# Sliding-window attention: the value matmuls with V stationary in two column halves, reciprocals spread by transfers

## The chip, the cores and the metric

The kernel runs on one core of a Trainium2 chip. The time is that of the whole program on the device, in microseconds (us); a kernel's time is the median of its runs.

## What is computed

One layer of a hybrid transformer for 2048 prompt tokens and 64 decode tokens, all in float32: input projections, latent attention (8 heads), sliding-window attention (8 query heads, 2 key/value heads of 64), output projection, and a convolutional feed-forward. The change touches the sliding attention alone:

```python
def swa_attend(q, k, v, bias, sinks, mask):
    s = jnp.einsum('bcqhgd,bckhd->bhgcqk', q, k).astype(jnp.float32) * SWA_SCALE + bias[:, :, None]
    if mask is not None:
        s = jnp.where(mask, s, NEG_INF)
    sink = sinks.astype(jnp.float32).reshape(SWA_KV_HEADS, SWA_GROUP, 1, 1, 1)
    m = jnp.maximum(jnp.max(s, axis=-1, keepdims=True), sink)
    e = jnp.exp(s - m)
    p = e / (jnp.sum(e, axis=-1, keepdims=True) + jnp.exp(sink - m))
    return jnp.einsum('bhgcqk,bckhd->bcqhgd', p.astype(v.dtype), v)
```

Each chunk of 64 queries sees its own 64 keys and the 128 before. The sum of the exponentials and the sink make the denominator of each query and head.

## The kernel before, in words

The program is a row of blocks: `project_inputs`, `window_attention`, `latent_attention`, `mix_and_ffn`. In each block every engine has a program of its own, written out by hand, and the engines meet at semaphores alone; a block begins when all engines have ended the one before.

`window_attention` (from line 781) walks over 17 tiles of queries: tiles 0 to 15 of 128 prompt tokens, tile 16 of the 64 decode tokens. A tile has 256 keys (192 for decode), in two halves of 128. Buffers of a tile alternate by its parity p. `walk` (line 852) sets the order on every engine: step t is `front(t)`, then `back(t-1)` (on ScalarE `back(t-1)`, then `front(t)`), and behind it `tail(t-2)`; steps 2 to 15 are a hardware loop of two steps and an unrolled pair.

- SP, `front`: loads queries, keys and V (transposed) of tile t+1, once the scores of tile t-1 and the turn of tile t's V are done. `tail`: stores a tile's output (line 918) once ScalarE has copied it.
- TensorE, `front` (line 950): scores of the 8 heads, queries stationary, 8 matmuls with 64 rows, in pairs in the upper and the lower half of the rows. Each fp32 matmul is two passes, which the profile lists as two instructions. `back` (line 974): in four groups g of two heads, four transposes of the probabilities each (into bank g % 2 of `tr`), and one group later the four value matmuls of the group (line 1002): the turned probabilities are stationary, V moves, 64 columns. Then V of the next tile is turned (line 972), and `tail` turns the finished output (line 1013).
- ScalarE, `front` (line 1024): eight exponentials with their sums (line 1028), one for the sink. `back` (line 1039): copies the four groups of turned probabilities from PSUM (line 1042), then the turned V (line 1037). `tail`: copies the turned output (line 1049).
- VectorE, `front` (line 1063): four instructions scale the scores and add the bias (line 1068), then the maximum (line 1076), its negative (1079) and the sink's offset (1082). `back`: denominator (1087), reciprocal (1089), and the product of values and reciprocals from PSUM (1092).
- GpSimd only sets constants (from line 938).

What waits for what around the change: `tr` has two banks and `ov`, `tt` one buffer each; the turned V and the turned output share `tt`. The product at 1092 waits for all value matmuls of a tile, and the next tile's value matmuls wait for it.

## Time and profile before

| | us |
|---|---|
| median of 3 runs (lowest, highest) | 2946.76 (2939.91, 2949.11) |
| the profiled execution's own time | 2937.64 |
| span of its trace, first to last instruction | 2935.8 |
| TensorE busy | 2773.2 (94%) |
| VectorE, ScalarE, GpSimd busy | 1888.1, 1316.3, 298.2 |
| mean granted clock of TensorE | 0.974 |
| sliding attention | 369.5 to 577 |

How to read the views: a row of the timeline begins with its start and its length in us (merged rows: from the first start to the last end), then engine, line, operation, output<-inputs, sizes and xcount; in brackets the time that the engine was idle before it and what ended that. PEld is TensorE's weight load, which overlaps PE. A row of the windows view has the stretch, its length, then busy time and (xcount) of PE, PEld, VectorE, ScalarE and GpSimd, the granted clock as a share of 2.4 GHz, the busy share of the DMA engines, and GB/s. A row of the source view has the least, the median and the greatest length in ns. A row of the DMA view has the bytes of one transfer and the median time from its issue to its landing in us.

### The profile page before, as it was taken

How to read it: one execution, taken by the hardware profiler on the slowest of the kernel's cores; microseconds unless marked ns; L12 is line 12 of the kernel's file. 1: busy time of each engine (PE TensorE's matmuls, PEld its weight loads, DVE VectorE, ACT ScalarE, POOL GpSimd, SP SyncE). 2: the span in 40 equal slices, each digit the busy share in tenths (PEclk: the TensorE clock that was granted, in tenths of full speed). 3: DMA queues.
4: the chain of work that ended last, by engine and by line, in shares of the span. 5: the costliest groups of instructions: out<-in, count | busy, mean ns of one | idle time of the engine just before them, and what ended most of it. 6: DMA issues, size and time to landing. Idle time of an engine off the chain costs nothing.

```text
span 2935.8 us, 43437 instructions
## 1 busy us (share of the span) xinstructions
PE 2773.2 (94%) x13872; PEld 2487.7 (85%) x13872; DVE 1888.1 (64%) x2662; ACT 1316.3 (45%) x2744; POOL 298.2 (10%) x336
## 2 busy tenths in 40 slices
PE   8999968799999998899999999999999999999996
PEld 7899857666666667799999989999899999999996
DVE  6777646466666673777647873487644876458743
ACT  5434246533333343464435444354434545346532
POOL 1111010000000001300010002100021101201002
PEclk9999979899999999999999999999999999999998
DMA  7566552313332213234333443335333353333432
GB/s 221 199 225 209 188 142 72 75 23 70 73 66 55 54 46 115 77 114 138 119 104 108 138 155 118 99 110 169 116 120 102 115 179 114 120 100 114 140 123 74
DMA packets 162016, 344.87 MB, mean 117 GB/s; under 512 B 41636, under 2 KB 105860, under 8 KB 160228
## 3 DMA queue, kind: packets, MB, share of 16 engines
q1 hardware_dynamic: 161892, 343.25, 38.7%
q8 instruction: 73, 1.20, 0.2%
q14 instruction: 51, 0.42, 0.0%
HBM read 288.83 MB, written 55.23 MB: 117 GB/s over the span
## 4 chain that ended last, share of the span: by engine, by line
PE 54%; DVE 2%; issue 2%; ACT 1%; DMA 1%; POOL 1%; SPq 0%; POOLq 0%; ACTq 0%; DVEq 0%
PE mf_acc L1877 53%; DVE mix_w_lo L2030 1%; ACT mix_w_hi L1923 1%; DMA mix_w_raw<-in_w_up 1%; POOL mf_ss L1835 1%; PE mf_st L1915 0%; DVE mf_x L2048 0%; DMA mix_w_raw<-in_w_out 0%; DVE mf_xn L2081 0%; DVE mf_x L2053 0%; POOL mf_y L1860 0%; DVE mix_a_lo L2086 0%; ACT mf_sq L1946 0%; ACT mf_sq L1980 0%; DVE mf_rstd L2065 0%
## 5 line engine op out<-in xcount | busy, mean ns | idle before, releaser
L2030 DVE TENSOR_TENSOR mix_w_lo<-mix_w_raw,mix_w_hi 128x1024 fp32r<-128x1024 f32 (+1 forms) x338 | 471.3, 1395 | 557.9 <-ACT mix_w_hi L1923 557.1
L1877 PE MATMUL mf_acc<-mix_a_hi,mix_w_hi 128*128 128x424 f32 (+1 forms) x2016 | 725.1, 360 | 29.3 <-DVE mix_a_lo L2060 8.8
L1877 PE MATMUL mf_acc<-mix_a_hi,mix_w_lo 128*128 128x424 f32 (+1 forms) x2016 | 718.6, 356 | 0.0
L1877 PE MATMUL mf_acc<-mix_a_lo,mix_w_hi 128*128 128x424 f32 (+1 forms) x2016 | 717.6, 356 | 0.0
L1923 ACT ACTIVATE mix_w_hi<-mix_w_raw 128x1024 fp32r<-128x1024 f32 (+1 forms) x338 | 382.2, 1131 | 520.4 <-PE mf_acc L1877 492.6
L1877 PEld LDWEIGHTS mf_acc<-mix_a_hi,mix_w_hi 128*128 128x128 f32 x2016 | 382.1, 190 | 45.0 <-issue 12.1
L1877 PEld LDWEIGHTS mf_acc<-mix_a_hi,mix_w_lo 128*128 128x128 f32 x2016 | 382.4, 190 | 10.8
L1877 PEld LDWEIGHTS mf_acc<-mix_a_lo,mix_w_hi 128*128 128x128 f32 x2016 | 382.3, 190 | 9.3 <-issue 0.7
L1345 PE MATMUL la_sc<-ahead_q,ahead_k 97*128 97x512 f32 (+5 forms) x1008 | 361.8, 468 | 0.0
L1877 PE MATMUL mf_acc<-mf_h_hi,mix_w_hi 128*128 128x424 f32 (+1 forms) x944 | 339.7, 360 | 6.8 <-DVE mix_w_lo L2030 3.9
L1877 PE MATMUL mf_acc<-mf_h_hi,mix_w_lo 128*128 128x424 f32 (+1 forms) x944 | 335.9, 356 | 0.0
L1877 PE MATMUL mf_acc<-mf_h_lo,mix_w_hi 128*128 128x424 f32 (+1 forms) x944 | 335.3, 355 | 0.0
L1407 ACT ACTIVATE la_prob<-la_sc 128x512 f32<-128x512 f32 (+1 forms) x336 | 174.1, 518 | 314.5 <-PE la_sc L1345 313.9
L1361 PE MATMUL la_ov<-la_prob,ahead_v 128*128 128x512 f32 (+5 forms) x672 | 293.5, 518 | 0.0
L1345 PEld LDWEIGHTS la_sc<-ahead_q,ahead_k 97*128 97x128 f32 (+1 forms) x1008 | 180.5, 189 | 128.5 <-issue 95.2
L1460 DVE TENSOR_REDUCE la_part<-la_sx 128x1 f32<-128x512 f32 (+5 forms) x328 | 184.6, 574 | 162.3 <-PE la_sx L1322 159.1
L1835 POOL TENSOR_TENSOR mf_ss<-mf_sq,mf_ss 128x424 f32<-128x424 f32 (+1 forms) x105 | 145.5, 1385 | 478.1 <-ACT mf_sq L1946 347.9
L1877 PEld LDWEIGHTS mf_acc<-mf_h_hi,mix_w_hi 128*128 128x128 f32 x944 | 178.3, 189 | 14.6 <-DVE mix_w_lo L2030 5.0
L1877 PEld LDWEIGHTS mf_acc<-mf_h_lo,mix_w_hi 128*128 128x128 f32 x944 | 178.2, 189 | 5.9 <-issue 1.7
L1877 PEld LDWEIGHTS mf_acc<-mf_h_hi,mix_w_lo 128*128 128x128 f32 x944 | 178.1, 189 | 4.2
L749 PE MATMUL pi_acc<-pi_x_hi,pi_w_hi 128*128 128x424 f32 (+1 forms) x400 | 148.0, 370 | 19.6 <-DVE pi_x_lo L528 14.5
L2104 DVE SCALAR_TENSOR_TENSOR mf_cv<-mf_u,mf_conv_w,mf_cv 128x424 f32<-128x424 f32 (+1 forms) x220 | 145.0, 659 | 32.5 <-DVE mf_cv L2101 28.9
(187 smaller groups left out, 3664.2 us busy)
## 6 DMA issues: line engine op xcount, KB each, us to landing
mix_w_raw<-in_w_up SPq DMA_DIRECT2D x220, 512.0 KB, 3.6
mix_w_raw<-in_w_down SPq DMA_DIRECT2D x80, 704.0 KB, 4.1
pi_w_raw<-in_w_in SPq DMA_DIRECT2D x49, 512.0 KB, 6.0
mix_w_raw<-in_w_out SPq DMA_DIRECT2D x40, 512.0 KB, 3.6
ahead_k<-kn_scr SPq DMA_DIRECT2D x8, 1120.0 KB, 14.8
ahead_q<-qn_scr SPq DMA_DIRECT2D x8, 1056.0 KB, 8.0
pi_x_raw<-in_x SPq DMA_DIRECT2D x4, 1696.0 KB, 11.4
qn_scr<-pi_ring SPq DMA_DIRECT2D x16, 424.0 KB
```

Of the source, the lines that this page charges most:

```text
L749: mm = pe.matmul(acc[:, g, 0:n], w[:, s, k], x[:, par, k, 0:n], start=(k == 0 and m == 0), stop=(k == KD - 1 and m == 2))
L1345: mm = pe.matmul(out, k[0:KR, p, a, c0:c0 + keys], q[0:KR, p, b, n0 + off:n0 + n], start=(term == 0), stop=(term == 2))
L1361: pe.matmul(ov[:, (5 * p + pos) % 2, off:n], v[0:keys, p, vt], prob[0:keys, (NKT * p + s) % RING, off:n], start=(m == 0), stop=(s == last_ ...
L1407: act.activation(prob[0:keys, (NKT * p + s) % RING, off:n], sc[0:keys, s % 3, off:n], ACT.Exp, scale=MLA_SCALE).then_inc(exp_done, 1)
L1460: op = dve.tensor_reduce(part[0:rows, par, t, slot:slot + 1], sx[0:rows, bank, 0:seen], AX_X, ALU.max)
L1835: pool.tensor_tensor(ss[:, kind, 0:n], sq[:, slot, 0:n], zeros[:, 0:n] if first else ss[:, kind, 0:n], ALU.add).then_inc(sq_added, 1)
L1877: mm = pe.matmul(acc[:, t_bank[0], 0:n], w[:, g, k], x[:, k, 0:n], start=(first and k == 0 and m == 0), stop=(last and k == count - 1 and ...
L1923: act.activation(w_hi[:, g, 0:count], w_raw[:, g, 0:count], ACT.Copy).then_inc(w_hi_made, 1)
L2030: dve.tensor_tensor(w_lo[:, g, 0:count], w_raw[:, g, 0:count], w_hi[:, g, 0:count].bitcast(F32), ALU.subtract).then_inc(w_split, 1)
L2104: dve.scalar_tensor_tensor(out=out, in0=u[:, g, 1:n + 1], scalar=conv_w[:, 1, bass.ds(f, 1)], in1=out, op0=ALU.mult, op1=ALU.add).then_inc ...
```

## The change

Cut to its core. Left out are semaphores that only change their names or are merged (`neg_done` and `off_done` into `shift_done`, and the like).

- Values: `values` at line 1005 of the new kernel makes a tile's output with four matmuls instead of sixteen. V is stationary, 128 keys by 64 columns, for key/value head g at columns 64g to 64g+63 of the array, and the turned probabilities of that head's four queries' heads move, 512 columns. The output comes out turned, [64g.., 4, 128], so the four output transposes and ScalarE's copy of them are gone.
- The turned probabilities are now grouped by key/value head and half, c = 2g + half, into bank `half` of `tr`. VectorE copies the first of the four groups (`keep_first`), ScalarE the other three.
- The reciprocals of a tile [128 queries, 8] are turned by TensorE into rows [8, 128], copied to SBUF by VectorE, written to DRAM by SP, and, when that has landed, read back twice with a step of 0 over 64 partitions (`spread`). VectorE copies the values from PSUM, and GpSimd multiplies them by the spread reciprocals (`scale`). `store` waits for that and is two transfers instead of one.
- TensorE's turn of the next V waits for `rec_kept`, VectorE's copy of the turned reciprocals, and `values` for `ov_kept`, VectorE's copy of the values before.

```diff
+            def spread(t, p, n):
+                sp.wait_ge(rec_kept, t + 1)
+                sp.dma_start(d["rec_scr"][p][:, 0:n], rec_rows[:, p, 0:n]).then_inc(rec_out[p], 16)
+                sp.wait_ge(rec_out[p], 16 * nth(t, p) + 16)
+                for g in range(2):
+                    row = bass.AP(tensor=d["rec_scr"].tensor, offset=(p * HEADS + g * SWA_GROUP) * P,
+                                  ap=[[0, SWA_DIM], [P, SWA_GROUP], [1, n]])
+                    sp.dma_start(rec_all[g * SWA_DIM:(g + 1) * SWA_DIM, p, :, 0:n], row).then_inc(rec_in[p], 16)
+
             def store(t, p, n):
-                sp.wait_ge(out_copied, t + 3)
+                sp.wait_ge(normed, t + 1)
                 cols = bass.ds(t * P, P) if n == P else slice(SEQ, TOK)
-                sp.dma_start(d["att_swa"][:, :, cols], outT[:, p, :, 0:n]).then_inc(att_out[p], 16)
-
-            def nothing(t, p, n):
-                pass
+                for g in range(2):
+                    sp.dma_start(d["att_swa_rows"][g][:, :, cols],
+                                 outT[g * SWA_DIM:(g + 1) * SWA_DIM, p, :, 0:n]).then_inc(att_out[p], 16)
...
+
+            def scale(t, p, n):
+                pool.wait_ge(ov_kept, t + 1)
+                pool.wait_ge(rec_in[p], 32 * nth(t, p))
+                if not (isinstance(t, int) and t == 0):
+                    pool.wait_ge(normed, t)
+                pool.tensor_tensor(outT[:, p, :, 0:n], outT[:, p, :, 0:n], rec_all[:, p, :, 0:n],
+                                   ALU.mult).then_inc(normed, 1)
+
+            pool.wait_ge(rows_set, 6)
+            walk(pool, nothing, scale, nothing)
+
...
             def turn_v(t, p, n):
                 if not (isinstance(t, int) and t == 0):
-                    pe.wait_ge(out_copied, t)
+                    pe.wait_ge(rec_kept, t)
                     pe.wait_ge(v_copied, t)
-                if not isinstance(t, int) or t > 0:
                     pe.wait_ge(qkv_in[p], 48 * nth(t, p) if n == P else 48 * (NT // 2) + 64)
                 pe.transpose(tt[0:n, 0, :], v_t[:, p, 0:n], ident[:]).then_inc(v_turned, 1)
 
+            def turn(t, p, n, g, half):
+
+                keys = DEC if half and n == DEC else P
+                for i in range(SWA_GROUP):
+                    mm = pe.transpose(tr[0:keys, half, i, 0:n],
+                                      prob[0:n, p, SWA_GROUP * g + i, half * P:half * P + keys], ident[0:n, 0:n])
+                mm.then_inc(tr_done, 1)
+
+            def values(t, p, n, half):
+
+                keys = DEC if half and n == DEC else P
+                src = ((v[:, 1 - p], v[:, p]) if n == P else (v_cache, v_new))[half]
+                for g in range(2):
+                    rows = slice(g * SWA_DIM, (g + 1) * SWA_DIM)
+                    mm = pe.matmul(ov[rows, :, 0:n], src[0:keys, rows], probT[0:keys, 2 * g + half, :, 0:n],
+                                   start=(half == 0), stop=(half == 1), skip_group_check=True)
+                if half:
+                    mm.then_inc(ov_done, 1)
+
             def back(t, p, n):
-                keys = (P, P if n == P else DEC)
-                for g in range(4):
-                    pe.wait_ge(exp_done, 8 * t + 2 * g + 2)
-                    pe.wait_ge(tr_copied, 4 * t + g + 1)
-                    for m in range(4):
-                        half = m % 2
-                        mm = pe.transpose(tr[0:keys[half], g % 2, m, 0:n],
-                                          prob[0:n, p, 2 * g + m // 2, half * P:half * P + keys[half]],
-                                          ident[0:n, 0:n])
-                    mm.then_inc(tr_done, 1)
-                    if g >= 1:
-                        values(t, p, n, keys, g - 1)
-                values(t, p, n, keys, 3)
+                pe.wait_ge(exp_done, 8 * t + 4)
+                pe.wait_ge(tr_copied, 3 * t + 2)
+                turn(t, p, n, 0, 0)
+                pe.wait_ge(tr_copied, 3 * t + 3)
+                turn(t, p, n, 0, 1)
+                pe.wait_ge(exp_done, 8 * t + 8)
+                pe.wait_ge(tr0_copied, t + 1)
+                turn(t, p, n, 1, 0)
+                pe.wait_ge(tr_copied, 3 * t + 4)
+                turn(t, p, n, 1, 1)
+                pe.wait_ge(v_copied, t + 1)
+                if not (isinstance(t, int) and t == 0):
+                    pe.wait_ge(ov_kept, t)
+                if n == DEC:
+                    pe.wait_ge(bias_in[1], 32)
+                pe.wait_ge(tr_copied, 3 * t + 5)
+                values(t, p, n, 0)
+                pe.wait_ge(tr_copied, 3 * t + 6)
+                values(t, p, n, 1)
+                pe.wait_ge(rec_done, 2 * t + 2)
+                pe.transpose(tt[0:HEADS, 1, 0:n], rec[0:n, p], ident[0:n, 0:n]).then_inc(rec_turned, 1)
                 if n == P:
                     turn_v(t + 1, 1 - p, P if not (isinstance(t, int) and t == NT - 1) else DEC)
 
-            def values(t, p, n, keys, g):
-                pe.wait_ge(tr_copied, 4 * t + g + 3)
-                if g == 0:
-                    pe.wait_ge(normed, t + 1)
-                    pe.wait_ge(v_copied, t + 1)
-                    if n == DEC:
-                        pe.wait_ge(vcache_in, 16)
-                for m in range(4):
-                    h, half = 2 * g + m // 2, m % 2
-                    kv = h // SWA_GROUP * SWA_DIM
-                    src = ((v[:, 1 - p], v[:, p]) if n == P else (v_cache, v_new))[half]
-                    mm = pe.matmul(ov[0:n, h], probT[0:keys[half], g, m, 0:n],
-                                   src[0:keys[half], kv:kv + SWA_DIM], start=(half == 0), stop=(half == 1))
...
-                pe.wait_ge(normed, t + 2)
-
-                pe.wait_ge(v_copied, NT + 1 if isinstance(t, int) and t > NT - 2 else t + 3)
-                pe.wait_ge(out_copied, t + 2)
-                for m in range(4):
-                    mm = pe.transpose(tt[:, m, 0:n], out[0:n, p, 2 * m:2 * m + 2].rearrange("p a b -> p (a b)"),
-                                      ident[0:n, 0:n])
-                mm.then_inc(out_turned, 1)
...
-            def keep_v(t, p, n):
+
+            def back(t, p, n):
                 act.wait_ge(v_turned, t + 1)
                 act.activation((v[:, p] if n == P else v_new)[0:n], tt[0:n, 0, :], ACT.Copy).then_inc(v_copied, 1)
-
-            def back(t, p, n):
-                for g in range(4):
-                    act.wait_ge(tr_done, 4 * t + g + 1)
-                    act.activation(probT[:, g], tr[:, g % 2], ACT.Copy).then_inc(tr_copied, 1)
-                if n == P:
-                    keep_v(t + 1, 1 - p, P if not (isinstance(t, int) and t == NT - 1) else DEC)
-
-            def tail(t, p, n):
-                act.wait_ge(out_turned, t + 1)
-                act.wait_ge(att_out[p], 16 * nth(t, p))
-                act.activation(outT[:, p, :, 0:n], tt[:, :, 0:n], ACT.Copy).then_inc(out_copied, 1)
-
-            walk(act, front, back, tail, back_first=True)
+                for c in range(1, 4):
...
+            def keep_first(t):
+                dve.wait_ge(tr_done, 4 * t + 1)
+                dve.tensor_copy(probT[:, 0], tr[:, 0]).then_inc(tr0_copied, 1)
 
...
                     dve.scalar_tensor_tensor(out=prob[0:n, p, h:h + 2, 0:keys], in0=sc[0:n, q, :, 0:keys],
                                              scalar=SWA_SCALE, in1=bias[0:n, p, h:h + 2, 0:keys],
                                              op0=ALU.mult, op1=ALU.add).then_inc(biased, 1)
+                if not (isinstance(t, int) and t == 0):
+                    keep_first(t - 1)
                 dve.wait_ge(biased, 4 * t + 8)
...
             def back(t, p, n):
+                if n == DEC:
+                    keep_first(t)
                 dve.wait_ge(exp_done, 8 * t + 8)
                 dve.wait_ge(sink_done, t + 1)
-                dve.tensor_tensor(den[0:n, p], total[0:n, p], sink_exp[0:n, p], ALU.add).then_inc(den_done, 1)
-                dve.wait_ge(den_done, t + 1)
+                dve.tensor_tensor(den[0:n, p], total[0:n, p], sink_exp[0:n, p], ALU.add).then_inc(rec_done, 1)
+                dve.wait_ge(rec_done, 2 * t + 1)
                 dve.reciprocal(rec[0:n, p], den[0:n, p]).then_inc(rec_done, 1)
-                dve.wait_ge(rec_done, t + 1)
+                dve.wait_ge(rec_out[p], 16 * nth(t, p))
+                dve.wait_ge(rec_turned, t + 1)
+                dve.tensor_copy(rec_rows[:, p, 0:n], tt[0:HEADS, 1, 0:n]).then_inc(rec_kept, 1)
                 dve.wait_ge(ov_done, t + 1)
-                dve.tensor_tensor(out[0:n, p], ov[0:n],
-                                  rec[0:n, p].rearrange("p (h o) -> p h o", o=1).broadcast_to([n, HEADS, SWA_DIM]),
-                                  ALU.mult).then_inc(normed, 1)
+                dve.wait_ge(att_out[p], 32 * nth(t, p))
+                dve.tensor_copy(outT[:, p, :, 0:n], ov[:, :, 0:n]).then_inc(ov_kept, 1)
...
+    d["rec_scr"] = nc.dram_tensor("rec_scr", (2, HEADS, P), F32, kind="Internal").ap()
+    d["att_swa_rows"] = [d["att_scr"][4 + 2 * g:6 + 2 * g].rearrange("k (e c) t -> c (k e) t", e=2) for g in range(2)]
```

The order of one step on TensorE, inside the loop (`wa_sc` scores, `wa_tr` turned probabilities, `wa_ov` values, `wa_tt` turned V, output or reciprocals). Before:

```order
L958 MATMUL wa_sc<-wa_k,wa_q 128x256 x4
...
L981 MATMUL wa_tr<-ahead_ident,wa_prob 128x128 x4
...
L1002 MATMUL wa_ov<-wa_vtok,wa_probT 128x64 x4
...
L981 MATMUL wa_tr<-ahead_ident,wa_prob 128x128 x4
...
L1002 MATMUL wa_ov<-wa_vtok,wa_probT 128x64 x4
L972 MATMUL wa_tt<-ahead_ident,wa_v 128x128
...
L1013 MATMUL wa_tt<-ahead_ident,wa_out 128x128 x4
```

Now:

```order
L982 MATMUL wa_sc<-wa_k,wa_q 128x256 x4
L1017 ISA
L1018 ISA
L1001 MATMUL wa_tr<-ahead_ident,wa_prob 128x128 x4
...
L1032 REGISTER_ALU
L1011 MATMUL wa_ov<-wa_probT,wa_vtok 64x512 x2
L1034 REGISTER_ALU
L1011 MATMUL wa_ov<-wa_probT,wa_vtok 64x512 x2
L1036 ISA
L1037 MATMUL wa_tt<-ahead_ident,wa_rec 8x128
L995 MATMUL wa_tt<-ahead_ident,wa_v 128x128
```

Before, groups of transposes and of values alternate and the output transposes end the step; now all sixteen transposes stand ahead of all values, and a turn of the reciprocals stands between the values and the turn of V.

The order of one step on VectorE, inside the loop, in the new kernel (`wa_rec_rows` turned reciprocals, `wa_outT` values to be multiplied):

```order
L1089 SCALAR_TENSOR_TENSOR wa_prob<-wa_sc,wa_bias 128x512
L1081 ISA
L1082 COPY wa_probT<-wa_tr 128x512
L1094 REGISTER_ALU
L1099 TENSOR_REDUCE wa_top<-wa_prob 128x8
...
L1112 TENSOR_TENSOR wa_den<-wa_total,wa_sink_exp 128x8
L1113 ISA
L1114 RECIPROCAL wa_rec<-wa_den 128x8
L1115 ISA
L1117 COPY wa_rec_rows<-wa_tt 8x128
L1119 REGISTER_ALU
L1120 COPY wa_outT<-wa_ov 128x512
```

The copy of the first group stands ahead of the maximum, and the two copies at the end stand where the product was (L1092 before).

The order of one step on SP's queue, inside the loop, in the new kernel:

```order
L893 DMA wa_q<-q_scr 128x4x128
L894 DMA wa_k<-k_scr 128x256
L895 DMA wa_v<-v_scr 128x128
L917 DMA rec_scr<-wa_rec_rows 8x128
L918 ISA
L922 DMA wa_rec_all<-rec_scr 64x512 x2
...
L928 DMA att_scr<-wa_outT 64x4x128
L928 ISA
L928 DMA att_scr<-wa_outT 64x4x128
```

Before, the three loads are followed by one store; now the write of the reciprocals, the wait for it, and the two reads stand between them.

## Rows read from the trace of the kernel before

**Rows 1.** Windows view, 20 us of the sliding attention in full swing

```profile
475.00:495.00 20.00, 16.56 (x139) 14.44 (x139) 12.33 (x20) 13.78 (x46) 0.00 (x0) 1.00 0.25 68
```

**Rows 2.** Timeline: starts of bias additions, and the next stage's first row

```profile
408.25 1.29 DVE L1068 SCALAR_TENSOR_TENSOR wa_prob<-wa_sc,wa_bias 128x512 f32<-128x512 f32 x2 [6.55 <-PE wa_sc L958]
...
468.85 2.48 DVE L1068 SCALAR_TENSOR_TENSOR wa_prob<-wa_sc,wa_bias 128x512 f32<-128x512 f32 x4 [1.49 <-PE wa_sc L958]
...
550.90 1.94 DVE L1068 SCALAR_TENSOR_TENSOR wa_prob<-wa_sc,wa_bias 64x384 f32<-64x384 f32 x4 [1.18 <-PE wa_sc L958]
...
577.05 0.18 POOL L1295 MEMSET la_part<- 128x24 f32 x2 [194.02 <-POOLq L786]
```

**Rows 3.** Timeline of ScalarE over one round

```profile
466.72 0.28 ACT L1037 ACTIVATE wa_vtok<-wa_tt 128x128 f32<-128x128 f32 x1 [1.31 <-PE wa_tt L972]
...
471.40 1.06 ACT L1042 ACTIVATE wa_probT<-wa_tr 128x512 f32<-128x512 f32 x2
...
473.62 0.60 ACT L1042 ACTIVATE wa_probT<-wa_tr 128x512 f32<-128x512 f32 x1 [1.16 <-PE wa_tr L981]
...
474.90 0.60 ACT L1042 ACTIVATE wa_probT<-wa_tr 128x512 f32<-128x512 f32 x1 [0.68 <-PE wa_tr L981]
...
476.81 0.28 ACT L1037 ACTIVATE wa_vtok<-wa_tt 128x128 f32<-128x128 f32 x1 [1.31 <-PE wa_tt L972]
```

**Rows 4.** Timeline of TensorE: the scores of tile 2, then one round

```profile
406.14 3.78 PE L958 MATMUL wa_sc<-wa_k,wa_q 64*128 64x256 f32 x16 [5.03 <-DMA wa_v<-v_scr]
...
467.05 0.66 PE L1013 MATMUL wa_tt<-ahead_ident,wa_out 128*128 128x128 f32 x4 [0.37 <-ACT wa_vtok L1037]
...
467.69 2.00 PE L958 MATMUL wa_sc<-wa_k,wa_q 64*128 64x256 f32 x16
...
472.86 0.48 PEld L981 LDWEIGHTS wa_tr<-ahead_ident,wa_prob 128*128 128x128 f32 x4
...
474.70 1.95 PE L1002 MATMUL wa_ov<-wa_vtok,wa_probT 128*128 128x64 f32 x16
...
476.38 0.20 PEld L972 LDWEIGHTS wa_tt<-ahead_ident,wa_v 128*128 128x128 f32 x1
```

**Rows 5.** Timeline of VectorE in the same round

```profile
471.37 2.29 DVE L1076 TENSOR_REDUCE wa_top<-wa_prob 128x8 f32<-128x2048 f32 x1
...
474.29 0.20 DVE L1089 RECIPROCAL wa_rec<-wa_den 128x8 f32<-128x8 f32 x1
...
476.76 0.69 DVE L1092 TENSOR_TENSOR wa_out<-wa_ov,wa_rec 128x512 f32<-128x512 f32 x1 [2.27 <-PE wa_ov L1002]
```

**Rows 6.** Timeline of TensorE in the latent attention, fp32 passes of 512 columns

```profile
710.18 1.02 PE L1361 MATMUL la_ov<-la_prob,ahead_v 128*128 128x512 f32 x2
...
711.97 0.59 PE L1361 MATMUL la_ov<-la_prob,ahead_v 128*128 128x512 f32 x1
```

**Rows 7.** Source view of line 554, VectorE's copies of 512 columns from PSUM

```profile
L554 DVE COPY pi_ring<-pi_ex x21: 680/683/692, 128.6 to 365.8; 106x512 f32<-106x512 f32 x16, 104x512 f32<-104x512 f32 x4, 128x512 f32<-128x512 f32 x1
```

**Rows 8.** Windows around the clock's fall; then the maximum's starts around it

```profile
533.00:534.00 1.00, 1.00 (x9) 1.00 (x8) 1.00 (x1) 0.01 (x1) 0.00 (x0) 0.70 0.84 236
...
529.80:532.60 2.80, 1.42 (x13) 0.89 (x9) 2.77 (x5) 2.80 (x12) 0.00 (x0) 1.00 0.00 0
...
531.86 2.29 DVE L1076 TENSOR_REDUCE wa_top<-wa_prob 128x8 f32<-128x2048 f32 x1
...
543.60 2.29 DVE L1076 TENSOR_REDUCE wa_top<-wa_prob 128x8 f32<-128x2048 f32 x1
```

**Rows 9.** DMA view, transfers like those that the change adds

```profile
wa_q<-q_scr SPq DMA_DIRECT2D x16, 256.0 KB, 2.9
...
ahead_v<-vt_scr SPq DMA_DIRECT2D x8, 16.0 KB, 10.5
...
att_scr<-la_att SPq DMA_DIRECT2D x8, 16.0 KB, 1.7
```

**Rows 10.** Source view of line 1835, GpSimd's sums of two inputs

```profile
L1835 POOL TENSOR_TENSOR mf_ss<-mf_sq,mf_ss x105: 1059/1104/2128, 1147.3 to 2912.3; 128x424 f32<-128x424 f32 x84, 128x416 f32<-128x416 f32 x21
```

More of the change, by code:

```diff
@@ L1007, in tail, with nothing @@
[L1007 to L1017 removed]
+            def nothing(t, p, n):
+                pass
```

78 lines of the change are left out of this document (40 added, 38 removed).

## The prediction

> **What bounds the kernel now.** I first looked for the stage that the change touches. The windows view [rows 1] gives the sliding attention in full swing: of 20 us TensorE has matmuls in flight for 16.6, ScalarE is busy 13.8 and VectorE 12.3, at a granted clock of 1.00. No engine is full, so the period of a tile is set by a ring of waits. The timeline of VectorE [rows 2] marks the tiles by the first of the four instructions that add the bias: tile 2 starts at 408.25, the last one (64 decode tokens) at 550.90, so 14 steps take 142.65 us, and the stage ends at 577.05 when the next one's first memset runs. Everything outside 408 to 577 I leave as it is.
>
> The ring is on ScalarE [rows 3]. The copy of the turned V starts in one round at 466.72 and in the next at 476.81: 10.09 us. Between them the eight exponentials run without a gap, then the copy of the output tile, then four copies of turned probabilities, before which ScalarE waits 1.16, 0.68 and, for the turned V, 1.31 us: 3.15 us idle per round. What it waits for is TensorE [rows 4], whose value matmuls are sixteen, one for each head and half of the keys, each in two fp32 passes with a stationary load: the last 16 of the 32 passes alone take 1.95 us. VectorE [rows 5] is waiting too (2.27 us before its product). So the present period is ScalarE's 6.9 us of work plus TensorE's share in between.
>
> **The change, part by part.** I follow one step of the new order, from the start of the bias additions to the next start, because VectorE now stands in three places of one ring: it copies the first turned quarter, it has to finish the reciprocals before TensorE may turn them, and TensorE may not turn the next V (same PSUM tile) before VectorE has taken the turned reciprocals away.
>
> 1. Bias additions to their end, 468.85 to 471.37 [rows 2, 5]: 2.52.
> 2. New: VectorE copies quarter 0 from PSUM, 128x512: 0.69 [rows 7]; it stands ahead of the 2.3 us maximum, and TensorE's quarter 2 reuses that bank, so it is on the path. Handing over 0.05.
> 3. TensorE turns quarter 2 (four transposes) until ScalarE starts: 472.86 to 473.62, 0.76 [rows 3, 4].
> 4. ScalarE copies it: 0.60 [rows 3]. Quarter 3 follows half a copy behind and is hidden by the first value matmuls. Handing over and changing the array's layout: 0.13.
> 5. The values. Before, 32 passes; now 8 passes of 512 columns. A pass of this kind in the latent attention takes 1.02 - 0.59 = 0.43 us from start to start [rows 6]. One after another, 8 take 3.44. If the two column halves run side by side, only the order of issue binds (first half's two passes, then its second beside the other's first): 5 x 0.43 = 2.15. I take 2.15, since the scores, whose two row halves are issued the same way, already do this: 16 passes of 256 columns in 2.00 us [rows 4], under 0.13 each, where half of 0.43 would be 0.215. No row shows column halves, so 3.44 stays as the upper end; nothing suggests less than 1.72. The Trainium skill (TensorEngine Tiling (Array Packing), Key Properties) says different tiles run independently; its TensorE: Matmul & The Clock Gate, Part 3, gives 2.38x for three column tiles. By that factor, taken as 1.6x for two, the term would be an estimated 2.2. The same page on tiling says that changing the layout drains the array; no row here isolates that.
> 6. TensorE turns the reciprocals (8 rows out): as the turned V, 476.38 to 476.81, 0.43 [rows 3, 4], and 0.07 for the pipe to run out: 0.50. They have been ready since about 6.3 us (2.52 + 0.69 + 471.37 to 474.29 + 0.20 [rows 5]), so values, not the reciprocal, are the later of the two.
> 7. VectorE's copy of 8 rows: 0.20, as the reciprocal [rows 5], and 0.05.
> 8. Turned V, then scores: four transposes and the change to scores took 0.64 (467.05 to 467.69), one takes about 0.33 [rows 4].
> 9. Scores to the next bias addition: 467.69 to 468.85, 1.16 [rows 2, 4].
>
> Sum 9.14, so 9.15 against 10.09. Removed and thus not in it: the four output transposes, the copy on ScalarE after the exponentials, VectorE's product (its place is taken by a plain copy of 0.69, hidden behind terms 8 and 9). ScalarE has about 5.9 us of work in the new round and waits for nobody long; its exponentials start when the maximum is ready (some 5.7 us in) and end 0.5 us after the next start, before quarter 2 asks for them.
>
> Beside the ring: SP now blocks on the small write of reciprocals before it issues the two spreading reads, the two stores and the next tile's loads. From the turned reciprocals I count the write's landing, then about 2.4 us of issuing, then 2.9 us until the queries have landed [rows 9], with waits and register work some 6.2 us on top of the landing. A 16 KB store lands in 1.7 us [rows 9]. Loads are made two tiles ahead, so two periods (18.3) must hold landing + 15.3: there is 1 us of slack with 1.7 to 2.0. GpSimd's product, 1.10 us for 424 columns [rows 10], so 1.3 for 512, is once per period on an idle engine, and its store is needed two tiles later: hidden. If that cover went it would add its 1.3 us to SP's queue, not to the ring.
>
> Start: nothing before 408.25 moves, as those scores wait for loads that SP issues late. The first step still has the low clock (its scores took 2.11 from 406.14 to 408.25, against 1.16 [rows 2, 4]), of which about +0.5 falls behind 408.25. Fourteen steps: 14 x 9.15 + 0.5 = 128.6, which is 14.0 less than 142.65. Tail, 26.15 us now [rows 2]: its value matmuls fall from 32 passes to 8 and the exponentials start earlier, but the last tile has to wait for the whole way of its reciprocals (1.7 + 0.9 + 2.9) and for GpSimd. I take -1, between -4 and +2. Together -15.0 with the clock held.
>
> **The clock.** Before, at 529.80 to 532.60 [rows 8] TensorE had nothing but eight transposes, as in each of the 14 rounds; once, the granted clock then fell (a mean of 0.70 between 533 and 534, so from 2.4 to 1.2 GHz inside it). Other rounds take 10.09, that one 11.74 (531.86 to 543.60 between two starts of the maximum [rows 8]), so a fall costs 1.65 us. In the new order the stretch without matmuls other than transposes is longer: from the end of the scores (0.45 after a start) to the values (4.75 after it), 4.3 us with sixteen transposes, instead of 2.6 us with eight. A fall will come more often; between 0 and 14 times. I take four, one of which the profile before has too, so three more: +5. Forecast: -10.
>
> **Against the runs.** The profiled execution took 2937.6 us, its span 2935.8; the median of three runs is 2946.8, 9 us above it. I apply the difference to the median: 2936.8 us. What a measurement of this kernel can tell from no change is 0.3%, 8.8 us, so the forecast lies just outside.
>
> **The rivals.**
> *The halves take turns.* If the column halves don't overlap, term 5 is 3.44 and the period 10.44: 14 x 1.29 = 18 more, +3 with the clock held, and about +8 with three falls. For it: no row shows column halves. Against it: the scores' row halves. About 2952.
> *The clock falls in most rounds.* Ten falls more: -15 + 16.5 = +1.5, 2948. For it: the longer stretch. Against it: 13 of 14 rounds kept the clock before.
> *The clock stays low.* The slower side. Where TensorE does not get back to the full clock in a round, its own terms double: term 3 by 0.4, the values by 2.15, the turns by 0.5, the scores by 0.95 (2.11 against 1.16, as above): about +4 a round. From six such rounds on (24 - 15 = +9) the kernel is slower; with seven, 2960. Against it: rounds with dense value matmuls should bring the clock back, as they did in the one round that took 11.74.
> *SP's queue.* If the write lands after more than 3 us, two periods are landing + 15.3: at 5 us the gain is gone (10.15 each), at 6 us the sum is +6. The worst small transfer, 16 KB behind others, took 10.5 us [rows 9], but the queue is nearly empty when this one is issued.
> *The change does what it says:* the rows of the program show it.
>
> **How the numbers follow.** Halves overlap and the clock falls at most seven times: 0.60, of which 0.45 with at most three more falls (faster) and 0.15 with four or more (within 0.3%). Most rounds fall: 0.10, within. Halves take turns: 0.16, of which 0.10 within and 0.06 slower. Clock stays low: 0.08, slower. SP's queue: 0.06, half within, half slower. Sum: faster 0.45, same 0.38, slower 0.17. The range goes from -18 (no fall, tail -4), 2929, to +10, 2957; the likeliest case alone spans 2929 to 2943. Left out are the low clock, the bad half of SP's queue and little else.
>
> **What would show it.** Starts of the bias additions 9.1 to 9.3 us apart where the clock is 1.00; the four pairs of value passes over in about 2.2 us (3.4 if they take turns); ScalarE's idle time before its copies mostly gone; VectorE waiting for the scores by under 1 us. Wrong would be: passes 0.43 apart through all eight, TensorE's wait before the scores ending on a DMA, or a clock of 0.5 in more than a third of the stage.

## The result, and the profile after

The kernel after takes 2913.33 us (median of 5 runs, 2911.83 to 2916.04) against 2945.41 (5 runs of the kernel before): a ratio of 0.990, interval 0.988 to 0.992. Four more runs of it gave 2905.88 to 2914.77, ratio 0.988 (0.987 to 0.990). Over all runs of this study the medians are 2912.1 (9 runs, 2905.9 to 2916.0) and 2941.4 (55 runs, 2933.7 to 2952.7): 29.3 us. The forecast was 2936.8, the range ended at 2929: the kernel gained more than the range allowed.

The table splits the profiled executions. A step is the time from the start of one tile's bias additions to the next; the tail goes from the start of the last tile's to the end of the stage.

| us | start of tile 2's additions | 14 steps | tail | from there to the end |
|---|---|---|---|---|
| before, four profiles | 408.25, 412.87, 409.75, 404.7 | 142.65, 142.72, 142.60, 142.86 | 26.15, 26.13, 26.2, 30.1 | 2358.8, 2358.0, 2360.9, 2368.1 |
| after, two profiles | 409.72, 407.40 | 122.64, 122.96 | 21.37, 20.20 | 2360.5, 2355.6 |

So the stage gives 25 us (20 in the steps, 5 in the tail). The other 4 of the 29.3 lie within what the first and last columns scatter between executions of one kernel. In the four profiles of the kernel before (2937.6 to 2947.5) the 14 steps differ by 0.3 us; the differences lie in the first and the last column and, once, in the tail.

The windows view of the kernel after, over nearly all of the stage (from 413.00, 3.3 us into the first step, to 541.00 in the tail) and in full swing (beside [rows 1]):

```profile
413.00:541.00 128.00, 95.06 (x615) 56.63 (x616) 100.94 (x177) 88.89 (x315) 17.83 (x14) 1.00 0.37 103
475.00:495.00 20.00, 15.33 (x97) 8.52 (x95) 15.88 (x29) 13.90 (x47) 3.31 (x3) 1.00 0.45 124
```

VectorE now has 15.88 busy in 20 us, more than any other engine. The clock is 1.00 in both stretches; the low clock at the start of the first step, which the kernel before has too, ends at 412.2. The timeline of VectorE (beside [rows 2, 5]), one step from 471.19 to 480.10, and the first and last marks of the stage:

```profile
409.72 1.29 DVE L1089 SCALAR_TENSOR_TENSOR wa_prob<-wa_sc,wa_bias 128x512 f32<-128x512 f32 x2 [5.11 <-PE wa_sc L982]
...
471.19 2.48 DVE L1089 SCALAR_TENSOR_TENSOR wa_prob<-wa_sc,wa_bias 128x512 f32<-128x512 f32 x4 [0.88 <-PE wa_sc L982]
473.59 0.68 DVE L1082 COPY wa_probT<-wa_tr 128x512 f32<-128x512 f32 x1
474.19 2.27 DVE L1099 TENSOR_REDUCE wa_top<-wa_prob 128x8 f32<-128x2048 f32 x1
...
477.08 0.20 DVE L1114 RECIPROCAL wa_rec<-wa_den 128x8 f32<-128x8 f32 x1
477.98 0.28 DVE L1117 COPY wa_rec_rows<-wa_tt 8x128 f32<-8x128 f32 x1 [0.70 <-PE wa_tt L1037]
478.19 0.67 DVE L1120 COPY wa_outT<-wa_ov 128x512 f32<-128x512 f32 x1
480.10 0.69 DVE L1089 SCALAR_TENSOR_TENSOR wa_prob<-wa_sc,wa_bias 128x512 f32<-128x512 f32 x1 [1.24 <-PE wa_sc L982]
...
532.36 1.95 DVE L1089 SCALAR_TENSOR_TENSOR wa_prob<-wa_sc,wa_bias 64x384 f32<-64x384 f32 x4 [0.69 <-PE wa_sc L982]
...
553.73 0.18 POOL L1321 MEMSET la_part<- 128x24 f32 x2 [3.25 <-POOLq L786]
```

The timelines of TensorE (beside [rows 4]) and ScalarE (beside [rows 3]) in that step:

```profile
474.42 1.06 PE L1001 MATMUL wa_tr<-ahead_ident,wa_prob 128*128 128x128 f32 x8 [1.37 <-DVE wa_probT L1082]
475.73 1.94 PE L1011 MATMUL wa_ov<-wa_probT,wa_vtok 128*64 128x512 f32 x8 [0.25 <-ACT wa_probT L1064]
477.60 0.27 PE L1037 MATMUL wa_tt<-ahead_ident,wa_rec 128*8 128x128 f32 x1
478.31 0.33 PE L995 MATMUL wa_tt<-ahead_ident,wa_v 128*128 128x128 f32 x1 [0.44 <-DVE wa_rec_rows L1117]
478.94 2.00 PE L982 MATMUL wa_sc<-wa_k,wa_q 64*128 64x256 f32 x16 [0.30 <-issue]
```

```profile
473.08 0.60 ACT L1064 ACTIVATE wa_probT<-wa_tr 128x512 f32<-128x512 f32 x1 [0.63 <-PE wa_tr L1001]
475.08 1.09 ACT L1064 ACTIVATE wa_probT<-wa_tr 128x512 f32<-128x512 f32 x2 [1.40 <-PE wa_tr L1001]
476.70 0.51 ACT L1054 ACTIVATE wa_prob<-wa_prob,wa_neg_top 128x256 f32<-128x256 f32 x1 [0.53 <-DVE wa_neg_top L1102]
```

The path is the predicted one: additions, VectorE's copy, quarter 2, its copy, values, the turned reciprocals, the turned V, scores. The reciprocals (ready at 477.28) come 0.3 us ahead of the values (TensorE turns them at 477.60). Eight value passes take 1.94 us: the halves run side by side. ScalarE still waits 0.63, 1.40 and 0.53 us in the step, 2.56 in all, against 3.15 before. Steps alternate between 8.55 and 8.91: every second one has 0.30 of issue time ahead of the scores, where the hardware loop branches. What lay beside the ring came out as [rows 7, 9, 10] had it:

```profile
wa_rec_all<-rec_scr SPq DMA_DIRECT2D x32, 128.0 KB, 2.9
...
L964 POOL TENSOR_TENSOR wa_outT<-wa_outT,wa_rec_all x17: 724/1273/1278, 411.3 to 549.8; 128x512 f32<-128x512 f32 x16, 128x256 f32<-128x256 f32 x1
```

These are the DMA view (the reads land in 2.9 us) and the source view of GpSimd's product (1.27).

### The profile page after: what moved, and what is told of

It reads as the page before. It is cut to its first block, busy times and chain, and to the rows that moved or that the text cites. A ratio compares the mean times of both kernels' runs of the same rounds, so it can differ in the third digit from the quotient of the medians.

```text
span 2914.2 us, 42679 instructions
## 1 busy us (share of the span) xinstructions
PE 2733.3 (94%) x13413; PEld 2422.1 (83%) x13413; DVE 1902.0 (65%) x2696; ACT 1299.8 (45%) x2710; POOL 320.3 (11%) x353
## 3 DMA queue, kind: packets, MB, share of 16 engines
q8 instruction: 71, 1.16, 0.2%
## 4 chain that ended last, share of the span: by engine, by line
PE 53%; DVE 3%; issue 2%; DMA 1%; ACT 1%; POOL 1%; SPq 0%; POOLq 0%; ACTq 0%; DVEq 0%
PE mf_acc L1903 53%; DMA mix_w_raw<-in_w_up 1%; DVE mix_w_lo L2056 1%; ACT mix_w_hi L1949 1%; POOL mf_ss L1861 1%; PE mf_st L1941 0%; DVE mf_x L2074 0%; DMA mix_w_raw<-in_w_out 0%; DVE mf_xn L2107 0%; DVE mf_x L2079 0%; POOL mf_y L1886 0%; DVE mix_a_lo L2112 0%; ACT mf_sq L1972 0%; ACT mf_sq L2006 0%; DVE mf_rstd L2091 0%
```

## The experiments

**The theory**: the halves overlap; the step is the ring above, and the transfers are hidden behind it. **The rivals**: the gain is the smaller number of passes; or the transfers or ScalarE hold the step.

**1. No overlap.**

```diff
-                    rows = slice(g * SWA_DIM, (g + 1) * SWA_DIM)
-                    mm = pe.matmul(ov[rows, :, 0:n], src[0:keys, rows], probT[0:keys, 2 * g + half, :, 0:n],
-                                   start=(half == 0), stop=(half == 1), skip_group_check=True)
+                    mm = pe.matmul(ov[:, :, 0:n], src[0:keys, :], probT[0:keys, 2 * g + half, :, 0:n],
+                                   start=(half == 0 and g == 0), stop=(half == 1 and g == 1), skip_group_check=True)
```

> Both head groups' value matmuls take the whole V tile (128 columns, both key heads) as stationary and add up in all 128 output rows, so no two of the eight passes can run side by side; the number of passes and of columns stays. (Each output row then holds the sum over both groups: the computation is changed here.) Theory: the two column halves overlap, and the period of a tile (8.76 us in the kernel after, 14 steps) is a ring on VectorE that the values just fit under. Then the eight passes take about 8 x 0.43 = 3.4 us from the first to the end instead of 1.94, the values become the later of the two things that the turned reciprocals wait for, the period rises to 10.2 to 10.4, and the kernel is 20 to 24 us slower than the kernel after, so about no faster than the kernel before. Rival: the gain came from having 8 passes instead of 32 and the overlap is worth nothing (the passes were hidden behind VectorE's maximum): then the period stays within 0.2 of 8.76 and the time within 3 us.

Measured: 2938.34 us (10 runs), ratio 1.000 (0.999 to 1.001), 25 above the kernel after; the 14 steps take 145.33. TensorE's timeline of one step:

```profile
462.11 1.07 PE L1001 MATMUL wa_tr<-ahead_ident,wa_prob 128*128 128x128 f32 x8 [1.37 <-DVE wa_probT L1081]
463.42 3.70 PE L1010 MATMUL wa_ov<-wa_probT,wa_vtok 128*128 128x512 f32 x8 [0.25 <-ACT wa_probT L1063]
466.96 0.27 PE L1036 MATMUL wa_tt<-ahead_ident,wa_rec 128*8 128x128 f32 x1
```

The same eight passes take 3.70 instead of 1.94. From their start to the turn of the reciprocals it is 3.54 (463.42 to 466.96) instead of 1.87 (475.73 to 477.60), and the steps take 10.22 and 10.58 instead of 8.55 and 8.91: the whole 1.67 reaches the step. The stage as a whole (145.33 and a tail of 23.97) is as long as in the kernel before (142.65 and 26.15), so without the overlap the change gains nothing. The rival falls.

**2. No transfers.** `spread` is empty, its waits are gone, and `rec_all` is set to 1.0 once:

```diff
-                sp.dma_start(d["rec_scr"][p][:, 0:n], rec_rows[:, p, 0:n]).then_inc(rec_out[p], 16)
-                sp.wait_ge(rec_out[p], 16 * nth(t, p) + 16)
...
-                    sp.dma_start(rec_all[g * SWA_DIM:(g + 1) * SWA_DIM, p, :, 0:n], row).then_inc(rec_in[p], 16)
+            pool.memset(rec_all[:], 1.0).then_inc(rows_set, 1)
```

> The write of the turned reciprocals and the two reads that spread them are left out; GpSimd multiplies by a tile of ones (so the output is not divided by the sum of the probabilities here). All else stays, the turn of the reciprocals and VectorE's copy of the eight rows included. Theory: the round trip of the reciprocals (write landing, reads, about 4.5 us) is hidden in the 14 steps and only the last tile pays for it. Then the period stays at 8.76 within 0.05 and the end of the stage comes 3 to 5 us earlier: 3 to 5 us in all. Rival: SP, which blocks on the small write, or the transfers' landing still hold the ring at its ends (the alternation of 8.55 and 8.91): then the steps shrink by 0.2 or more each and the gain is 7 us or more.

Measured: 2907.4 us (4 runs); steps of 8.48 and 8.84 (120.63 in all, 2.0 less), tail 16.03 (5.3 less). VectorE's timeline of one step, the start of the last additions and the end of the stage:

```profile
469.03 2.48 DVE L1083 SCALAR_TENSOR_TENSOR wa_prob<-wa_sc,wa_bias 128x512 f32<-128x512 f32 x4 [0.88 <-PE wa_sc L976]
477.87 0.69 DVE L1083 SCALAR_TENSOR_TENSOR wa_prob<-wa_sc,wa_bias 128x512 f32<-128x512 f32 x1 [1.24 <-PE wa_sc L976]
...
529.08 1.01 DVE L1083 SCALAR_TENSOR_TENSOR wa_prob<-wa_sc,wa_bias 64x384 f32<-64x384 f32 x2 [0.61 <-PE wa_sc L976]
...
545.11 0.17 POOL L1314 MEMSET la_part<- 128x24 f32 x2 [3.24 <-POOLq L786]
```

The transfers cost 0.07 us in a step of the loop, 0.5 in the first step, 0.7 in the last and 5.3 in the tail. That is somewhat more than the 3 to 5 expected, and nearly all of it at the ends: in the loop SP and the landings don't hold the ring.

**3. ScalarE copies all four quarters** (`for c in range(4)` in its `back`; `keep_first` and `tr0_copied` are gone).

> ScalarE copies all four groups of turned probabilities, VectorE none (the split of the change undone alone). Theory: VectorE's copy of group 0 stands in the ring between the bias additions and the turn of group 2. Without it group 2 is turned as soon as ScalarE has copied group 0, and VectorE's maximum starts 0.6 us earlier: the period falls from 8.76 to about 8.2 and the kernel gains 14 x 0.55 = 7 to 8 us. Rival: ScalarE was the bound before and becomes it again, since it gets 0.6 us more work ahead of the group that the values wait for: then the period goes back to 9.1 to 9.4 and the kernel loses 5 to 9 us.

Measured: 2900.12 us (4 runs, 2898.06 to 2903.22), ratio 0.987 (0.985 to 0.989), 13 below the kernel after. Timelines of TensorE and of VectorE in one step:

```profile
467.20 1.94 PE L1010 MATMUL wa_ov<-wa_probT,wa_vtok 128*64 128x512 f32 x8 [0.20 <-ACT wa_probT L1063]
469.42 0.27 PE L1036 MATMUL wa_tt<-ahead_ident,wa_rec 128*8 128x128 f32 x1 [0.28 <-DVE wa_rec L1105]
```

```profile
463.75 2.48 DVE L1084 SCALAR_TENSOR_TENSOR wa_prob<-wa_sc,wa_bias 128x512 f32<-128x512 f32 x4 [0.92 <-PE wa_sc L981]
466.26 2.29 DVE L1092 TENSOR_REDUCE wa_top<-wa_prob 128x8 f32<-128x2048 f32 x1
...
469.16 0.20 DVE L1105 RECIPROCAL wa_rec<-wa_den 128x8 f32<-128x8 f32 x1
```

Most steps take 7.84 or 8.17, 112.69 in all: 9.95 less, where 7 to 8 was expected. The values start 3.45 after the additions instead of 4.54, so 1.09 earlier, and now the reciprocals are the later (TensorE waits 0.28 for them): the two paths had been 0.3 us apart, and shortening both moves the step by what the second allows. VectorE's copy, one part of the change, costs 10 us in the steps. The rival, ScalarE, falls: in the trace it still waits 1.15 us for the maximum.

**4. Reciprocals turned one step later**, the stores behind them on SP:

```diff
                 turn(t, p, n, 0, 1)
+                pe.wait_ge(v_copied, t + 1)
+                if not (isinstance(t, int) and t == 0):
+                    turn_rec(t - 1, 1 - p, P)
...
                     keep_first(t - 1)
+                if not (isinstance(t, int) and t < 2):
+                    keep_rec(t - 2, p, P)
...
+            def late(t, p, n):
+                if not (isinstance(t, int) and t < 2):
+                    store(t - 2, p, P)
+                if not (isinstance(t, int) and t == 0):
+                    spread(t - 1, 1 - p, P)
```

> The kernel after, with the reciprocals of a tile turned one step later (behind the turn of quarter 1 of the next tile), so that TensorE goes from the values straight to the turn of the next V and to the scores; VectorE takes the turned rows behind its copy of quarter 0, and the transfers that spread them, GpSimd's product and the stores come one step later. Theory: the ring of the kernel after runs through VectorE alone: bias additions, copy of quarter 0, maximum, sum, reciprocal, their turn, VectorE's copy of 8 rows, turn of V, scores (8.76). With the reciprocals out of it the next limit is bias additions 2.40, copy 0.60, turn of quarters 2 and 3 and the values until 6.5, turn of V, scores to the first addition 1.2: 7.8 to 8.1, so 10 to 13 us less than the kernel after (about 2901 to 2903). Rival: the reciprocals only hide the values, or the 1.2 us from scores to additions is set by the loads: then the period falls by under 0.2 and the time by under 3 us.

> The late turn of the reciprocals together with ScalarE's copying of all four quarters. Theory: each alone shortens the ring on VectorE, and together they leave ScalarE's round (eight exponentials 3.9, sink 0.1, copy of V 0.25, four copies 2.4: 6.7) plus its waits as the limit: a period of 7.1 to 7.5, 9 to 13 us less than with ScalarE's copies alone (2900), so 2887 to 2891. Rival: the two gains are the same gain, since in both cases TensorE's own chain (four turns and values after the exponentials, turn of V, scores) ends the round at 7.8 to 8.0: then the time is 2897 to 2903.

Measured: 2917.01 and 2911.76 us (4 runs each), where 2901 to 2903 and 2887 to 2891 were expected: both misses. With VectorE's copy, steps 2 to 4 take 7.83 or 7.84 as the theory has it, but from the sixth on 8.5 to 9.7 (120.54 in all). With ScalarE's copies the second and third take 7.66 and 7.52, from the fifth on 8.4 to 9.1 (117.37 in all). The tails are 26.6 and 27.1. Two views of one such step of the first version, SP's queue and VectorE:

```profile
465.70 0.45 SPq L919 DMA_DIRECT2D rec_scr<-wa_rec_rows  x1
467.50 1.15 SPq L924 DMA_DIRECT2D wa_rec_all<-rec_scr  x2
...
473.33 1.53 SPq L930 DMA_DIRECT2D att_scr<-wa_outT  x2
474.92 0.49 SPq L919 DMA_DIRECT2D rec_scr<-wa_rec_rows  x1
```

```profile
465.45 0.20 DVE L1142 RECIPROCAL wa_rec<-wa_den 128x8 f32<-128x8 f32 x1
467.39 0.69 DVE L1147 COPY wa_outT<-wa_ov 128x512 f32<-128x512 f32 x1 [1.75 <-DMA att_scr<-wa_outT]
```

SP goes round in 9.22 us from write to write: its store waits for GpSimd's product, which waits for the reads, and the next write stands behind the store. VectorE's copy of the output then waits 1.75 for a store to land. Two suspects were left: what stands behind GpSimd's product (SP's next write and, through the store, VectorE's copy), or the transfers as such. The clock was a third: this profile has three falls in the steps, the first at 464.3.

**5. The same, GpSimd issuing the stores behind its product** (written into `rec_all`, so that the output tile is free once multiplied):

```diff
+                pool.tensor_tensor(rec_all[:, p, :, 0:n], outT[:, p, :, 0:n], rec_all[:, p, :, 0:n],
                                    ALU.mult).then_inc(normed, 1)
...
+                    pool.dma_start(d["att_swa_rows"][g][:, :, cols],
+                                   rec_all[g * SWA_DIM:(g + 1) * SWA_DIM, p, :, 0:n]).then_inc(att_out[p], 16)
```

> The late turn of the reciprocals once more, but GpSimd itself issues the stores behind its product (into the tile of spread reciprocals, so that VectorE's copy of the next output no longer waits for a store to land), and SP only loads and spreads. What the version with the stores on SP showed: the first five steps took 7.83 to 8.03 us, the later ones 8.5 to 9.7, and there SP went round in 9.2: write, 1.8 until it had landed, reads, 3.2 until they had landed, product 1.28, stores 1.5, next write. Theory: SP's queue, which stood in order behind GpSimd's product, was the new bound. Then all 14 steps now take 7.8 to 8.0, 109 to 112 us in place of 120.5, and the kernel 2900 to 2905. Rival: it is the transfers themselves (landing slower when more are under way) or the lower clock that three rounds had: then the later steps stay at 8.5 or more and the time at 2911 or more.

> The same with ScalarE copying all four quarters. In the version with the stores on SP the first steps took 7.5 to 7.7 and the later ones 8.4 to 8.7. Theory: with SP out of the way all steps take 7.2 to 7.7, 101 to 108 us, so the kernel stands 5 to 11 us below ScalarE's copies alone (2900): 2889 to 2895. Rival: ScalarE's 6.7 us of work with its waits for TensorE end at 8.0 as in ScalarE's copies alone: then 2900 again.

Measured: 2905.29 and 2901.27 us (4 runs each), ratios 0.987 (0.985 to 0.988) and 0.985 (0.983 to 0.986). VectorE's timeline of one step of the first version:

```profile
474.54 2.48 DVE L1109 SCALAR_TENSOR_TENSOR wa_prob<-wa_sc,wa_bias 128x512 f32<-128x512 f32 x4 [0.62 <-PE wa_sc L986]
...
482.37 2.48 DVE L1109 SCALAR_TENSOR_TENSOR wa_prob<-wa_sc,wa_bias 128x512 f32<-128x512 f32 x4 [0.61 <-PE wa_sc L986]
```

With VectorE's copy every step from the second to the twelfth takes 7.83 or 7.84 (109.78 in all), as expected: the ring without the reciprocals is what the terms say, and the transfers as such don't stretch it. The edit does two things at once: it takes the stores out of SP's order and frees the output tile sooner. What each is worth was not told apart. There is no fall of the clock in the steps here; three at 1.65 us would make 5 of the 10.8 us between the two versions, so the clock alone doesn't explain it.

With ScalarE's copies the steps from the fourth to the twelfth take 7.45 to 7.55 (105.94 in all), as expected. The total was not: 2889 to 2895 was forecast, and 2901.27 can't be told from experiment 3 (2900.12, ratio 0.987). Its steps are 6.7 us shorter, but the tail takes 25.6 us instead of 22.1 (the last reciprocals set out later), and the profiled execution was 4 us later at the start and 5 longer behind the stage, which is the scatter of the table. All runs of experiment 3 and of this second version (2898.1 to 2904.4) lie below all of the kernel after. Those of the first (2904.4 to 2908.2) overlap with it in time, though its stage is 9 us shorter. Experiment 3 is the simplest of the three.

**6. Runs of the kernel before again, and its clock.**

> The kernel before, unchanged, for a second profile of it. The two profiled executions stand 21.6 us apart in span, the medians 32. Theory: the granted clock of the sliding stage differs from one execution of the kernel before to the next; each fall costs 1.65 us, and the profile of before showed one. Then this profile shows another number of falls, and its total differs from 2937.6 by about 1.65 us for each. Rival: the scatter of the kernel before (2934 to 2949) lies in the other stages: then the 14 steps take 142.65 within 1 us again, and the difference stands before or behind the stage.

> The kernel before again, one look for the clock of its sliding stage. The runs of the kernel before range from 2934 us at a mean granted clock of 0.974 to 2953 at 0.968. Theory: the runs differ in how often the clock falls in the 14 rounds, and one fall takes 3.2 us at 0.50 and costs 1.65 us; a run of 2940 has some three falls, one of 2947 some seven. Rival: what differs is the start of the stage (408.25 in one profile, 412.87 in the other) and the later stages, and the number of falls is always one.

> The same as the look before it: the number of rounds longer than 11 us should follow the total time (about one more per 1.65 us above 2934 to 2936) by the theory, and stay at one by the rival.

Measured: 2941.55, 2941.26 and 2947.51 us, with one fall of the clock in the 14 steps each time (a step of 11.74, 11.45 and 11.77), wherever the total stood; the theory that the number of falls in the steps makes the scatter falls. The 6 us between the last two lie in the tail (+3.9) and behind the stage (+7.2), less an earlier start (-5.1), as the table has them. The longer tail does go with the clock: it turned low 3.7 us after the last tile's additions had begun (at 551.3), against 13.2 us in the first profile (at 564.1).

> The kernel before with eight more transposes of the identity (1.09 us) in the 1.38 us that TensorE waits in every round for the first copy of turned probabilities; their result is overwritten. Theory: a fall of the clock needs this pause (each of the four profiles of the kernel before has exactly one fall, in round 8, 15, 15 or 16, right behind it). Then no round takes over 10.3 us, the 14 steps take 141.0 instead of 142.65, and the time falls by 1 to 3 us. Rival: the pause has nothing to do with it, since the other 13 rounds have the same pause and keep the clock: then one round of 11.7 remains, and the time is that of the kernel before.

```diff
+                    if g == 1:
+                        pe.wait_ge(normed, t + 1)
+                        for _ in range(8):
+                            pe.transpose(ov[0:P, 0:2, :].rearrange("p a b -> p (a b)"), ident[:], ident[:])
```

TensorE's pause in the kernel before, just ahead of the fall of [rows 8]; its timeline of one step of this version; and the windows view over the steps from 412.00 on:

```profile
532.58 1.25 PE L1002 MATMUL wa_ov<-wa_vtok,wa_probT 128*128 128x64 f32 x8 [1.38 <-ACT wa_probT L1042]
```

```profile
472.92 1.04 PE L988 MATMUL wa_ov<-ahead_ident 128*128 128x128 f32 x8
474.42 1.10 PE L1006 MATMUL wa_ov<-wa_vtok,wa_probT 128*128 128x64 f32 x8 [0.46 <-ACT wa_probT L1046]
```

```profile
412.00:561.00 149.00, 136.00 (x1143) 120.60 (x1139) 90.14 (x149) 100.55 (x332) 0.00 (x0) 1.00 0.23 64
```

With the pause cut from 1.38 to 0.46 there is no fall, and the steps take 140.73 (141.0 expected). The time is 2939.05 (9 runs), ratio 0.998 (0.997 to 0.9995). One profile without a fall, against four with one, speaks for the pause as a condition, and no more. It is not enough for a fall: the kernel after has a pause of 1.37 in nearly every step and no fall in the steps of two profiles, and so have experiments 1 and 2 in one profile each. The version of experiment 4 (VectorE's copy) has three falls, two of them behind pauses of 2.07 and 2.60. What decides among rounds with the same pause stays open.

> The kernel after again, for a second profile and more runs. Theory: its 14 steps take 122.6 within 0.2 with no fall of the clock, and its tail 21.4; what scatters between executions (start of the stage, the stages behind it) is the same as before. Then the median lies at 2911 to 2916 and the difference to the kernel before, over all runs, at 25 to 28 us, not the 32 of the first medians. Rival: the change also shortens a later stage by some us: then the part behind the stage is under 2357 here too, against 2358 to 2368 in the kernel before.

Measured: 2909.88 us (4 runs), 1 us under the range expected; steps 122.96 (0.36 above 122.6, not within 0.2), tail 20.20 (1.2 shorter), no fall. The difference over all runs came out at 29.3, above the 25 to 28 expected. The part behind the stage took 2355.6 in this profile, under the 2357 that the rival had named, and 2360.5 in the first. Four profiles of the kernel before have 2358.0 to 2368.1. So a gain of 3 or 4 us in a later stage is neither shown nor excluded.

## Why the prediction was wrong

The path of the step was right: the halves overlap, and the transfers are hidden. What failed was the clock, whose falls never came, and the sizes of the steps' terms, of the tail and of the base. The range already had room for no fall and for a tail of -4 (it ended at -18, 2929). So the 15.7 us by which the result lies below it come from the base (5.4), the terms of the step (6.0), 0.8 of the tail, and some 3 of scatter outside the stage. The step, by the prediction's terms, from the rows above (the long step):

| term | predicted | measured |
|---|---|---|
| 1 additions | 2.52 | 2.40 (471.19 to 473.59) |
| 2 VectorE's copy and handing over | 0.74 | 0.83 (to 474.42) |
| 3 turn of quarter 2 | 0.76 | 0.66 (to 475.08) |
| 4 ScalarE's copy and handing over | 0.73 | 0.65 (to 475.73) |
| 5 values | 2.15 | 1.87 (to 477.60) |
| 6 turn of the reciprocals | 0.50 | 0.38 (to 477.98) |
| 7 VectorE's copy of 8 rows | 0.25 | 0.33 (to 478.31) |
| 8 turned V | 0.33 | 0.63 (to 478.94), 0.25 in the short step |
| 9 scores to additions | 1.16 | 1.16 (to 480.10) |
| sum | 9.15 | 8.91, short step 8.55; mean of the 14: 8.76 |

- **Term 5** is the largest miss: 0.28. I took five passes of 0.43, one half's start behind the other's. The two halves start together, so that the four pairs take 1.87 to the next instruction. The Trainium skill (TensorEngine Tiling (Array Packing), Key Properties) has different tiles run independently, and the pair 3.70 to 1.94, a factor of 1.91, agrees. The factor 1.6 that I had worked out from the 2.38 of its TensorE: Matmul & The Clock Gate was too low. Terms 1, 3, 4 and 6 are each 0.1 too long. For term 1 I took the time until the maximum starts, which waits for the additions to end; the copy that now follows starts 0.08 before that end (473.59 against 473.67). For terms 3 and 6 I counted from a weight load, which starts 0.11 before its matmul (472.86, 472.97). For term 4 I put 0.13 for the handing over; about 0.05 is left of it. In all 0.39 a step, so 14 x 0.39 = 5.5 us, with the 0.5 for the low clock at the start 6.0 (128.6 against 122.6).
- **The clock** is the step whose mechanism failed: "A fall will come more often", of which "I take four". There was none in 14 rounds, in either profile. Three more falls were priced at +5. (The sum of 128.6 already stood without any fall, so four falls should have been +6.6: a slip of its own.) I took a stretch with nothing but transposes for the cause. That stretch did grow, from 2.5 us (530.11 to 532.58) to 3.8 (471.95 to 475.73) with sixteen transposes, and it brought nothing. That is 5 us. The rivals on the clock had 0.18 between them and rest on the same cause, which nothing here bears out. What makes a fall stays open.
- **The tail** was taken at -1 and came out at -4.8 and -5.9. The wait for the last reciprocals was seen rightly (experiment 2: 5.3 us). What I missed is how much the fewer passes are worth there, since the decode tile's values run at the half clock in both kernels: the 32 passes and the turns between them took 7.65 us (564.04 to 571.69), the 8 that replace them 2.1 (542.25 to 544.35). The timeline and the windows view (clock 0.50), before and after:

```profile
564.04 0.43 PE L1002 MATMUL wa_ov<-wa_vcache,wa_probT 128*64 128x64 f32 x2 [2.37 <-ACT wa_probT L1042]
...
571.69 1.11 PE L1013 MATMUL wa_tt<-ahead_ident,wa_out 128*128 128x128 f32 x4
...
564.50:571.50 7.00, 7.00 (x38) 5.02 (x38) 0.00 (x0) 1.19 (x2) 0.00 (x0) 0.50 0.14 39
```

```profile
542.25 1.12 PE L1011 MATMUL wa_ov<-wa_probT,wa_vcache 128*64 128x256 f32 x4
...
544.35 0.27 PE L1037 MATMUL wa_tt<-ahead_ident,wa_rec 64*8 64x64 f32 x1
...
542.00:544.00 2.00, 1.91 (x10) 0.62 (x8) 0.00 (x0) 0.70 (x2) 0.22 (x1) 0.50 0.74 211
```

- **The base.** The forecast was set on the median of three runs, 2946.8; over 55 runs the kernel before takes 2941.4. That is 5.4 of the 23.5 us between 2936.8 and 2913.3. The others: 6.0 by the step, 5 by the clock, 3.8 by the tail; some 3 remain to the scatter outside the stage.
- **ScalarE** "waits for nobody long" was wrong: it waits 2.56 of 8.91 us, and its idle time is not "mostly gone". It is off the path, so the forecast didn't suffer, but the sign would have misled: the copy that the change moved to VectorE had room here (experiment 3).
- **SP's queue** was right: 1.2 us from the write's issue to the reads' (544.96 to 546.14 for the last tile), hidden (experiment 2). Experiment 4 shows what the rival feared: with the next write behind a store that waits for GpSimd, the queue's round of 9.22 us is longer than the ring.
- **The halves take turns** (0.16, 2952): if they had, the kernel would stand at 2938.

## What to carry to other kernels

Read terms from start to start of the rows that will stand there, and keep what a ring leaves as slack beside it: here two paths ended 0.3 us apart, and giving VectorE a copy that ScalarE had room for cost 10 us. A transfer's round trip in the middle of a ring was cheap here as long as the next round's issue did not stand behind a wait on its consumer. And a base of three runs of a kernel that scatters by 19 us is itself a term of the range.

## What the hardware showed unexpectedly

Two column halves of the array, fp32, 512 columns moving, run side by side: eight passes in 1.94 us against 3.70 with all columns.

Going over from full-array transposes to column halves costs nothing that shows: the values start 1.31 us after the turn of quarter 2 in both (474.42 to 475.73, and 462.11 to 463.42 in experiment 1). TensorE waits 0.25 us for ScalarE there in both, so a shorter cost could be hidden. The way back has no such wait, and takes 0.1 us longer: from the last value passes to the turn of the reciprocals it is 0.53 us behind column halves, 0.43 behind full columns (the kernel after, then experiment 1):

```profile
477.07 0.60 PE L1011 MATMUL wa_ov<-wa_probT,wa_vtok 128*64 128x512 f32 x2
477.60 0.27 PE L1037 MATMUL wa_tt<-ahead_ident,wa_rec 128*8 128x128 f32 x1
```

```profile
466.53 0.59 PE L1010 MATMUL wa_ov<-wa_probT,wa_vtok 128*128 128x512 f32 x1
466.96 0.27 PE L1036 MATMUL wa_tt<-ahead_ident,wa_rec 128*8 128x128 f32 x1
```

And the granted clock fell exactly once in the 14 steps in each of four profiles of the kernel before, but not in the one profile where TensorE's pause was filled, nor in the two of the kernel after and those of experiments 1 and 2, where it was just as long ([rows 8] show the fall, the windows view above its absence).
